# Eighteen weight slots of the feed-forward layers as seven block products, with the sums on VectorE

## The reference

```python
def swiglu(h, w_gu, w_down):
    gate, up = jnp.split(h @ w_gu, 2, axis=-1)
    return (jax.nn.silu(gate) * up) @ w_down

def sublayer(x, shift, scale, gate, g_pre, g_post, fn, res_weight):
    h = rmsnorm(x, g_pre) * (1 + scale[:, None, :]) + shift[:, None, :]
    return x + res_weight * gate[:, None, :] * rmsnorm(fn(h), g_post)
```

## Time and profile before

| | us |
|---|---|
| median of 3 runs (lowest, highest) | 2746.37 (2745.3, 2747.19) |
| the profiled execution | 2743.05 |
| its span, first to last instruction | 2741.3 |
| TensorE busy in the span | 2435.3 (89%) |
| VectorE busy in the span | 1781.5 (65%) |
| gate and up slots 1 to 10, stages 0, 2, 4, 6 | about 138.3 each |

### The profile page before, as it was taken

The page is one execution under the profiler, slowest core; times in us unless marked ns, Lnnn a source line. Parts: engine busy times, 40 slices in busy tenths (PEclk is TensorE's granted clock), DMA queues, the critical chain, the costliest instruction groups (busy, mean ns, idle before and its releaser), DMA issues. The chain is left out here.

```text
span 2741.3 us, 26967 instructions
## 1 busy us (share of the span) xinstructions
PE 2435.3 (89%) x9731; PEld 1555.4 (57%) x9731; DVE 1781.5 (65%) x3934; ACT 620.4 (23%) x1778; POOL 681.0 (25%) x698
## 2 busy tenths in 40 slices
PE   8999999999999999999998977968879788877776
PEld 6874558857884688668654523734446544432222
DVE  4566744485557545654797876687887878874444
ACT  2001210001000210000233333332333523332222
POOL 1110100110100011100344444343445444443432
PEclk9999999999999999999999999988999989999999
DMA  9775926774784368865899999999999999999997
GB/s 384 307 297 205 390 97 242 310 280 184 298 320 175 132 241 338 317 273 222 333 418 421 419 422 420 421 406 418 416 422 402 421 416 412 421 409 422 421 422 321
DMA packets 120524, 931.61 MB, mean 340 GB/s; under 512 B 15133, under 2 KB 16565, under 8 KB 20422
## 3 DMA queue, kind: packets, MB, share of 16 engines
q0 software_dynamic: 94032, 670.65, 60.0%
q1 hardware_dynamic: 26358, 259.23, 23.7%
HBM read 928.74 MB, written 1.09 MB: 339 GB/s over the span
## 5 line engine op out<-in xcount | busy, mean ns | idle before, releaser
L1376 PE MATMUL psF<-ring,p_diag 128*128 128x512 f32 x1792 | 870.9, 631 | 234.3 <-ACT p_diag L1822 234.3
L2703 DVE SCALAR_TENSOR_TENSOR ring<-ring,h 128x1024 f32<-128x1024 f32 x512 | 620.8, 1223 | 340.5 <-DMA ring<-in_peer_uv_dram,lamt 337.2
L718 POOL DMA_INDIRECT ring<-in_peer_uv_dram,lamt x512 | 588.5, 1150 | 961.0 <-PE psF L1376 759.7
L1376 PEld LDWEIGHTS psF<-ring,p_diag 128*128 128x128 f32 x1792 | 339.0, 199 | 695.3 <-ACT p_diag L1822 351.9
L1026 PE MATMUL psR<-hT,ring 128*128 128x256 f32 x2560 | 553.2, 379 | 0.0
L1026 PEld LDWEIGHTS psR<-hT,ring 128*128 128x128 f32 x2560 | 486.1, 190 | 65.9
L1813 ACT ACTIVATE small<-small 128x2 f32<-128x2 f32 x255 | 51.8, 203 | 808.7 <-DVE ring L2703 808.4
L2266 DVE TENSOR_TENSOR arena<-arena,psR 128x256 f32<-128x256 f32 x80 | 33.7, 421 | 266.1 <-ACT arena L1683 266.1
L546 POOL DMA_DIRECT2D mring<-in_mod_t_dram x80 | 42.5, 532 | 651.9 <-DVE mring L2091 650.5
L1683 ACT ACTIVATE arena<-psR 128x256 f32<-128x256 f32 x86 | 32.9, 383 | 567.9 <-PE psR L1026 521.9
L1822 ACT ACTIVATE p_diag<-ident,small 128x128 f32<-128x128 f32 x446 | 158.2, 395 | 8.3
(11 more groups left out here) (373 smaller groups left out, 2710.5 us busy)
## 6 DMA issues: line engine op xcount, KB each, us to landing
ring<-in_gu_t_dram SPq DMA_DIRECT2D x44, 2048.0 KB, 9.3
mring<-in_mod_t_dram POOLq DMA_DIRECT2D x80, 1024.0 KB, 7.0
M<-in_mod_t_dram POOLq DMA_DIRECT2D x40, 1024.0 KB, 7.1
ring<-in_down_t_dram SPq DMA_DIRECT2D x20, 2048.0 KB, 9.0
mring<-in_tail_w_dram SPq DMA_DIRECT2D x40, 1024.0 KB, 9.3
ring<-in_conv_in_t_dram SPq DMA_DIRECT2D x12, 2048.0 KB, 8.5
ring<-in_gla_in_t_dram SPq DMA_DIRECT2D x6, 2048.0 KB, 9.6
ring<-in_out_t_dram SPq DMA_DIRECT2D x6, 2048.0 KB, 9.2
```

What stands on the lines that cost most here:

```text
L718: pool.indirect_dma_start(out=pair(n % PAIRS), out_offset=None, in_=rows, in_offset=bass.IndirectOffsetOnAxis(ap=s_idx[:, c:c + 1], axis=0 ...
L1376: ins = pe.matmul(psF[:, b, f * HALF:(f + 1) * HALF], p_diag[:, n % PAIRS, :], row_v(n % PAIRS)[:, f * HALF:(f + 1) * HALF], start=(i == 0 ...
L2703: dve.scalar_tensor_tensor(row_u(c), row_u(c), 1.0, h[:, b, :], ALU.mult, ALU.mult, accum_out=p_dots[:, c:c + 1]).then_inc(dot_done, 1)
```

## The change

A slot's product is [gate; up] = W^T hT with W cut in 2 x 2 blocks: 4 and 4 tiles of the 1024 rows, gate and up columns; hT is cut in the same halves of rows and in its two blocks of 128 tokens. In 18 slots (`SEVEN_SLOTS`: slots 2, 4, 6, 8, 10 of stages 0, 2 and 6, slots 2, 4, 6 of stage 4) the eight block products are replaced by seven, each of 2 x 4 matmuls of 128 x 128. That is 56 matmul instructions of 128 x 128 where 32 of 128 x 256 stood.

VectorE makes, once a stage, four sums of `hT` blocks (`sum_turned`, 128 x 512), and for each such slot four sums of weight blocks (`sum_slot`, 128 x 1024; the second makes `slot_summed` 1, the third, in place, 2, the fourth 3). It collects the products: `sum_four` (four instructions of 128 x 256) and `mix` (one of 128 x 512 in PSUM, and the two multiplications).

Each such slot s + 1 goes with the plain slot s before it. TensorE: first unit of s; products 1, 6, 5, 7 (`first_four`); second unit of s; products 3, 4, 2 (`last_three`). Products go to the halves of `psF` in turn. VectorE: `sum_slot(s + 1)`; multiplication 2s; half steps; `sum_four`; half steps; multiplication 2s + 1; `acts(s)`; `mix`; `acts(s + 1)`; the half steps of both tiles of slot s + 1. The load of `ln` on GpSimd's queue moves from the middle of the conditioning loads to behind them, with a wait for the last `sum_slot` to be read, because its place is used.

```diff
+SEVEN_SLOTS = {0: (2, 4, 6, 8, 10), 2: (2, 4, 6, 8, 10), 4: (2, 4, 6), 6: (2, 4, 6, 8, 10)}
+SEVENS = [(n, s) for n in SEVEN_SLOTS for s in SEVEN_SLOTS[n]]
+TURNED_SUMS = {0: 12544, 2: 7168, 4: 14 * T, 6: 6144}
+LAST_SUM = {0: 6144, 2: 6144, 4: 13440, 6: 12560}
...
+    def slot_sum(st, m):
+        if m < 2:
+            return h_flat[:, m * 4 * T:(m + 1) * 4 * T].rearrange("p (k n) -> p k n", k=4)
+        return view(LAST_SUM[st.n], 4, T)
+    def turned_sum(st, m):
+        return view(TURNED_SUMS[st.n] + m * 4 * P, 4, P)
+    def seven_bank(st, s, product):
+        half = psF[:, (SEVEN_SLOTS[st.n].index(s) + 1) % 2, :]
+        at = {1: 0, 6: T, 5: 2 * T, 7: 3 * T, 2: 0, 3: 2 * T, 4: 3 * T}[product]
+        return half[:, at:at + T]
...
-            if piece == (7, 4):
-                pool.wait_ge(x_ready, x_count(6))
-                for j, name in enumerate(("ln_g_2", "ln_b_2")):
-                    pool.dma_start(ln[:, j, :], a[name][0, 0:1, :].to_broadcast([P, D])).then_inc(conv_ln_loaded, 16)
...
+        pool.wait_ge(last_sum_read, len(SEVENS))
+        for j, name in enumerate(("ln_g_2", "ln_b_2")):
+            pool.dma_start(ln[:, j, :], a[name][0, 0:1, :].to_broadcast([P, D])).then_inc(conv_ln_loaded, 16)
...
+            def seven(s, product):
+                w = slot(st.w + s, KD, HALF)
+                lhs, rhs = {1: (w[:, 0:4, 0:T], hT[:, 0:4, 0:P]), 2: (w[:, 4:8, 0:T], hT[:, 4:8, 0:P]),
+                            3: (slot_sum(st, 2), hT[:, 4:8, P:]), 4: (w[:, 4:8, T:], turned_sum(st, 3)),
+                            5: (slot_sum(st, 0), turned_sum(st, 0)), 6: (slot_sum(st, 1), turned_sum(st, 1)),
+                            7: (w[:, 0:4, T:], turned_sum(st, 2))}[product]
+                ps = seven_bank(st, s, product)
+                for c in range(2):
+                    for k in range(4):
+                        ins = pe.matmul(ps[:, c * P:(c + 1) * P], lhs[:, k, c * P:(c + 1) * P], rhs[:, k, :],
+                                        start=(product in (1, 5) and c == k == 0), stop=(k == 3), skip_group_check=True)
+                return ins
+            def first_four(s):
+                e = SEVENS.index((st.n, s))
+                arrived(st.w + s)
+                if s == SEVEN_SLOTS[st.n][0]:
+                    have(st.u + 5)
+                seven(s, 1)
+                pe.wait_ge(turned_summed, list(SEVEN_SLOTS).index(st.n) + 1)
+                pe.wait_ge(slot_summed, 3 * e + 1)
+                seven(s, 6)
+                seven(s, 5).then_inc(slot_sums_read, 1)
+                pe.wait_ge(slot_summed, 3 * e + 2)
+                seven(s, 7).then_inc(four_products, 1)
+            def last_three(s):
+                e = SEVENS.index((st.n, s))
+                pe.wait_ge(four_summed, e + 1)
+                pe.wait_ge(slot_summed, 3 * e + 3)
+                seven(s, 3).then_inc(last_sum_read, 1)
+                seven(s, 4).then_inc(unit_full, 1)
+                seven(s, 2).then_inc(unit_full, 1)
...
-            have(u - 2)
+                if s in SEVEN_SLOTS[st.n]:
+                    continue
+                arrived(st.w + s)
+                gate_up(s, 0)
+                if s + 1 in SEVEN_SLOTS[st.n]:
+                    first_four(s + 1)
+                gate_up(s, 1)
+                if s + 1 in SEVEN_SLOTS[st.n]:
+                    last_three(s + 1)
+            have(st.u + (23 if 10 in SEVEN_SLOTS[st.n] else 24))
             down(st)
...
+                if j // 2 in SEVEN_SLOTS[st.n]:
+                    if j % 2 == 0:
+                        e = SEVENS.index((st.n, j // 2))
+                        act.wait_ge(slot_mixed, e + 1)
+                        have(n - 1)
+                        act.activation(sg[:, :, P:], by_unit(seven_bank(st, j // 2, 3)), ACT.Silu).then_inc(gate_ready, 1)
+                        full(n + 1)
+                        act.activation(sg[:, :, 0:P], by_unit(seven_bank(st, j // 2, 2)), ACT.Silu).then_inc(gate_ready, 1)
+                    continue
...
-                if j % 2 == 0:
-                    dve.wait_ge(unit_stored, u - 1)
-                    sum_acts(st, j // 2 - 1)
-                for _ in range(halves_done(st, j) - halves_done(st, j - 1)):
-                    half_step()
-                if st.n == 0 and j == FT // 2:
+            def acts(s):
+                dve.wait_ge(unit_stored, st.u + 6 + 2 * s)
+                sum_acts(st, s)
+            def halves(j):
+                half_steps(halves_done(st, j) - halves_done(st, j - 1))
+            acts(0)
+            for s in range(1, 11):
+                if s in SEVEN_SLOTS[st.n]:
+                    continue
+                if s + 1 in SEVEN_SLOTS[st.n]:
+                    sum_slot(st, s + 1)
+                gate_up(2 * s)
+                halves(2 * s)
+                if st.n == 0 and s == 5:
                     tables()
-                if j == FT - 2:
-                    sum_weights(st, 0)
+                if s + 1 in SEVEN_SLOTS[st.n]:
+                    sum_four(st, s + 1)
+                    halves(2 * s + 1)
+                    if s == 9:
+                        sum_weights(st, 0)
+                    gate_up(2 * s + 1)
+                    acts(s)
+                    mix(st, s + 1)
+                    if s < 9:
+                        acts(s + 1)
+                        halves(2 * s + 2)
+                        halves(2 * s + 3)
+                else:
+                    if s == 10:
+                        sum_weights(st, 0)
+                    gate_up(2 * s + 1)
+                    halves(2 * s + 1)
+                    if s < 10:
+                        acts(s)
+            if 10 in SEVEN_SLOTS[st.n]:
+                halves(20)
+                halves(21)
+            full(st.u + 25)
             sum_weights(st, 1)
-            dve.wait_ge(unit_stored, u)
-            sum_acts(st, PAIRED - 1)
+            acts(10)
...
+        def sum_turned(st):
+            dve.wait_ge(unit_stored, st.u + (5 if st.n else 4))
+            b11, b12, b21, b22 = [hT[:, k:k + 4, b * P:(b + 1) * P] for k in (0, 4) for b in range(TB)]
+            t1, t2, t3, t4 = [turned_sum(st, m) for m in range(4)]
+            link(dve.tensor_tensor(t1, b12, b11, ALU.subtract))
+            link(dve.tensor_tensor(t2, b22, t1, ALU.subtract))
+            dve.tensor_tensor(t3, b22, b12, ALU.subtract)
+            dve.tensor_tensor(t4, b21, t2, ALU.subtract).then_inc(turned_summed, 1)
+        def sum_slot(st, s):
+            e = SEVENS.index((st.n, s))
+            i = st.w + s
+            w = slot(i, KD, HALF)
+            a11, a12, a21, a22 = w[:, 0:4, 0:T], w[:, 4:8, 0:T], w[:, 0:4, T:], w[:, 4:8, T:]
+            s1, s2, s4 = [slot_sum(st, m) for m in range(3)]
+            dve.wait_ge(w_loaded[home_of(i)], landed[i])
+            if s != SEVEN_SLOTS[st.n][0]:
+                dve.wait_ge(last_sum_read, e)
+            link(dve.tensor_tensor(s1, a21, a22, ALU.add))
+            dve.tensor_tensor(s2, s1, a11, ALU.subtract).then_inc(slot_summed, 1)
+            dve.tensor_tensor(a21, a11, a21, ALU.subtract).then_inc(slot_summed, 1)
+            dve.wait_ge(slot_summed, 3 * e + 1)
+            dve.tensor_tensor(s4, a12, s2, ALU.subtract).then_inc(slot_summed, 1)
+        def sum_four(st, s):
+            e = SEVENS.index((st.n, s))
+            sum_16, sum_165 = macc[:, 1, 0:T], macc[:, 1, T:]
+            p1, p6, p5, p7 = [seven_bank(st, s, m) for m in (1, 6, 5, 7)]
+            dve.wait_ge(four_products, e + 1)
+            link(dve.tensor_copy(sum_16, p1))
+            link(dve.tensor_tensor(sum_16, p6, sum_16, ALU.add))
+            link(dve.tensor_tensor(sum_165, p5, sum_16, ALU.add))
+            dve.tensor_tensor(sum_165, p7, sum_165, ALU.add).then_inc(four_summed, 1)
+        def mix(st, s):
+            e = SEVENS.index((st.n, s))
+            full(st.u + 4 + 2 * s)
+            both = psF[:, (SEVEN_SLOTS[st.n].index(s) + 1) % 2, HALF:].rearrange("p (m n) -> p m n", m=2)
+            dve.tensor_tensor(both, both, macc[:, 1, 0:T].unsqueeze(1).to_broadcast([P, 2, T]), ALU.add)\
+                .then_inc(slot_mixed, 1)
+            dve.wait_ge(slot_mixed, e + 1)
+            dve.wait_ge(four_summed, e + 1)
+            for b, up in ((1, macc[:, 1, T:]), (0, seven_bank(st, s, 4))):
+                dve.wait_ge(gate_ready, t_gate.next())
+                dve.tensor_tensor(actT[:, 2 * s:2 * s + 2, b * P:(b + 1) * P], sg[:, :, b * P:(b + 1) * P],
+                                  by_unit(up), ALU.mult).then_inc(unit_stored, 1)
...
```

More of the change, by code:

```diff
@@ L327, in _program @@
     weights_summed = sem("weights_summed")
+    turned_summed = sem("turned_summed")
+    slot_summed = sem("slot_summed")
+    slot_sums_read = sem("slot_sums_read")
+    last_sum_read = sem("last_sum_read")
+    four_products = sem("four_products")
+    four_summed = sem("four_summed")
+    slot_mixed = sem("slot_mixed")
     weights_sums_used = sem("weights_sums_used")
@@ L945, in down @@
```

(33 more changed lines are left out.)

5 lines of the change are left out of this document (3 added, 2 removed).

## The result

The changed kernel takes 2757.24 us (median of 6 runs, 2753.64 to 2759.26) against 2745.84 us (6 runs, 2744.15 to 2747.19): ratio 1.0036, 95% interval 1.0026 to 1.0047, so 7 to 13 us more. The profiled execution took 2757.21 us; its span, first to last instruction, is 2755.3 us against 2741.3. The forecast was 2751.5 us, 5.1 more than before, with a range of 2739 to 2763.

What follows compares the result with a forecast made beforehand. TensorE was taken to bound gate and up, with VectorE half free but its order deciding. 2743.05 - 21.5 + 19.6 + 7.0 = 2748.15 us, plus 3.3 for the median: 2751.5 us, range 2739 to 2763.

Steps and rivals of the forecast that it cites:

- What TensorE saves: Gate and up: seven narrow products take 12.63 us a slot for 13.83, saving 1.19 us, 21.5 us for 18 slots.
- Rival 2: Gate and up: narrow 128 x 128 matmuls run at 0.240 us in groups with waits between; 13 us more, 2764.5; 12%.
- The stall at the second product: Gate and up: product 6 waits for weight sums behind half steps, 1.14 or 1.54 us a pair; 19.6 us together.
- The seam to down: Start of down: one more half step ahead of pair 1's weight sums in stages 0, 2 and 6; costs 7.0 us.
- The rest at nothing: `mix`, slot freeing and loading, `ln`'s load and half-step loads cost nothing; without load cover, 1 to 2 us a pair.
- rival 4: Gate and up: half steps or slots wait for late loads, 1.5 us for 13 pairs, 20 us, 2771; 4%.
- Rival 3: VectorE's weight sums take 1.4 us for 1.22, their source in runs of 256; 4.7 us over the stalls, 2756; 10%.
- Rival 5: Gate and up: change fails, e.g. stalls bring TensorE's lower clock, up to twice the time; far above range, 2%.
- Rival 1: Gate and up: VectorE has the first two weight sums ready for product 6, only the seam is lost; 2731.9; 12%.

Runs made afterwards that it cites:

- e1: The changed kernel with the weight sums of the next pair (sum_slot) moved ahead of the half steps: 2735.63 us, ratio 0.9964 to the kernel before.
- e5: e3 with the half steps of tile 21 moved behind pair 1's weight sums and slot 10's sums, in all four stages: 2719.12 us, ratio 0.9902 to the kernel before.
- e4: The kernel before, without products by seven, with only tile 20's half steps moved behind the last multiplication in stages 0, 2 and 6: 2757.61 us, ratio 1.0038.
- e2: The changed kernel with tile 20's half steps moved from the end of gate and up to ahead of pair 0's weight sums: 2744.91 us, ratio 0.9997 to before.
- e3: The changed kernel with both the edits of e1 and e2: 2728.66 us, ratio 0.994 to the kernel before.

## Why the prediction was right, and what it mis-sized

The sign of the net effect, the place of both losses and the time within its range came out; the size was 5.1 us, measured 11.4 by the medians (14.0 by the spans of the two profiles, by which the terms below are counted). In part that is luck: 3.5 us more than forecast were won in gate and up, and 12.6 more than forecast were lost behind it.

- **What TensorE saves**: forecast 1.19 us a slot, 21.5 in all. Measured 1.31 a slot (27.63 less 26.32), 23.5 in all. Besides, pair 0 of down no longer waits 0.4 us, which gives 0.55 us a stage, 2.2 in all. e1 and e5 get 24 to 25 us in gate and up. Rival 2 (0.240 us) is out: 0.223.
- **The stall at the second product**: forecast a loss of 1.54 (linked half steps) and 1.14 us (unlinked); measured 27.84 less 26.32 = 1.52 and, from 103.34 to 130.78, 27.44 less 26.32 = 1.12. The pair with one half step and the first pairs of stages 2, 4 and 6 have none. Stage 0's first idles 0.56 us at product 6 and 0.20 at product 1, and costs 1.4 us in all (gate and up of e1: 132.98 us in stage 0, 131.60 in stage 2; forecast 0.9). The idle time alone is 0.89 to 1.64 us in the 13 later pairs, less than what each loses. All stalls together cost 20.4 us, forecast 19.6. So gate and up of the four stages, forecast 1.9 us shorter, is about 5.4 shorter: 2.0 from the better saving and 2.2 from pair 0, less 0.8.
- **The seam to down**: forecast 2.25, 2.25 and 2.49 us and nothing in stage 4. Measured 2.65, 2.65, 3.04 and 0.63. Pair 0 starts 0.55 us earlier, but pair 1 when VectorE is ready: what gate and up gains there the seam takes.
- **The term that was mis-sized** is that of the seam, 7.0 us, priced as idle time alone. It measured 9.0 us idle and 3.2 at the lower clock right behind it (stages 2 and 6), 12.2 in all. I gave the lower clock 2%, for the stalls in the pairs, where it never came: idle times up to 1.64 us, clock 1.00. It came behind the longer ones. e4 has this term apart from the products: 11.5 us by the medians.
- **The rest at nothing** held for `mix` and the slots (gate and up shows no other idle time, but for the 0.20 us at product 1), not for the loads of half steps. In gate and up, where rival 4 had them late, VectorE waited for none; in stage 1 it waited 10.7 us for them where it waited 2.1 before. 4.4 us of rest 0 beside the seam's are there, part of it chance.
- Rival 3 (slower VectorE instructions) is out: the weight sums take 1.22 us, as the additions of the earlier trace rows did. Rival 5 is out for gate and up: granted clock 1.00.
- Rival 1 (VectorE keeps ahead) was wrong for the order as written, and right for VectorE's capacity: e1 makes it true by moving four instructions.

## What to carry to other kernels

A helper engine with half its time free still sets the pace if the work that the busy engine waits for stands behind work that nobody waits for: walk its queue from the moment of the hand-over, and put first what is asked for first. The same holds at the end of a stage, and there a stop of TensorE can cost more than its length, since it may come back at the lower clock (stage 2: 2.65 us idle, 1.5 more behind it). Test the two halves of a change apart: here some 20 us of real gain were hidden by one order and some 11 us by one call of half steps in the wrong place.

## What the runs showed of the hardware that I had not expected

The clock. After idle times of 0.56 to 1.64 us, at most once a pair, the granted clock of gate and up stayed 1.00 in every profile. At the seams one idle time had both outcomes. After 2.65 to 2.73 us the clock fell in 10 of the 14 seams of all profiles (stage 2 of the changed kernel in both, e1 and e4) and not in 4 (stage 0 of the changed kernel's first profile, of e1 and of e4, stage 4 of e2). After 3.11 us in stage 6 of e3 it stayed at 1.00, and after 5.1 to 5.2 us in stage 6 it fell all four times. It isn't new with the change either: in the kernel before it fell behind the 2.10 us of stage 4 in both profiles, and not behind the 2.10 us of stage 6. Before, stage 4:

```profile
824.98 3.64 PE L935 MATMUL psR<-hT,arena 128*128 128x512 f32 x4 [2.10 <-DVE hT L2311]
```

```profile
825.00:829.00 4.00, 4.00 (x6) 1.70 (x7) 3.41 (x8) 0.00 (x0) 0.00 (x0) 0.57 0.82 344
```

What a fall costs: four records of 128 x 512 took 3.54 us to the next start behind the 5.14 us of stage 6 in the changed kernel, and 1.80 at a granted clock of 1.00 behind the 3.11 us of e3. What decides between the two outcomes no run here shows, nor how much of the spread between executions it makes: the changed kernel's six runs lie 5.6 us apart, the six of before beside them 3.0, but the fifteen of before beside e1 to e4 6.5.
